# One of four weight combinations of a crossed MLP unit: accumulating transfer in place of a VectorE subtraction

## The chip, the cores and the metric

The kernel runs on one core of one Trainium2 chip. The metric is the device time of one execution in microseconds, median of several runs; smaller is better.

## What is computed

One block of a hybrid encoder on a sequence of 256 tokens with a model width of 2048: normalisation, one wide projection, a two-directional state-space branch and an attention branch, a gated merge, and then an MLP:

```
h2 = rms_norm(x, g_mlp)
x  = x + jnp.square(jax.nn.relu(h2 @ w_mlp_in)) @ w_mlp_out      # 2048 -> 8192 -> 2048
return rms_norm(x, g_final)
```

Everything is float32. The change touches only the product with `w_mlp_out` (8192 x 2048).

## The kernel before

**Pieces and blocks.** All weights stream from HBM in pieces of 128 partitions x 1024 floats (512 KB). SyncE (SP) issues the loads in one order (L610), in the MLP into a ring of seven raw buffers (`raw` and the second half of `gates`). For each block of weights ScalarE (ACT) writes a rounded copy, the high part, into `whi` or `whi_late` (L637), and VectorE (DVE) writes what is left, the low part, into `wlo` or `wlo_late` (L1022). TensorE (PE) then makes three products: high x high, high x low, low x high (L1719 to L1721; in the first MLP product, L1728 and L1732). There are eight slots for high and low parts, so ACT can be at most seven blocks ahead of PE: it waits on `used`, which PE increments after each block.

**The MLP.** The 8192 hidden columns are taken in four groups g. In each group four windows `mlp_in` make 2048 hidden columns, then windows `mlp_pair` multiply them into the output columns: q = 0 is the first half of the output columns, q = 1 the second; in the last group q = 1 is replaced by two plain windows. A column pair (g, q) has four units, each of 2 x 2 weight pieces: b11, b12, b22, b21 in load order. An ordinary unit has four blocks of 12 matmuls each. A **crossed** unit does the product of the 2 x 2 blocks with seven products in place of eight (Strassen's scheme in Winograd's form): the blocks are b11, b22, t1, b21, t3, t2, t4 (`PAIR_BLOCKS`), of six matmuls each, and t1 to t4 are combinations of the pieces:

```
t1 = b12 - b11    t3 = b22 - b12    t2 = b22 - t1    t4 = b21 - t2
```

`CROSSED` names the crossed units: units 1 and 2 with q = 0; units 0, 1 and 2 with q = 1. That makes 4 x 2 + 3 x 3 = 17 crossed units. With q = 1 the order is: half of unit 3, unit 0, unit 1, a quarter of unit 3, unit 2, the last quarter of unit 3.

DVE makes the four combinations (`difference`, L1025), in place, between its low parts; t1 overwrites b11, t3 overwrites b12, t2 overwrites b22, t4 overwrites b21. The order of DVE in a unit is: low b11, t1, low b22, t3, low t1, t2, low b21, t4, low t3, low t2, low t4. ACT makes the high parts in block order; before that of a combination it waits for `t_made`. The order on each engine is written out: `DUE` says at which step which block's parts are made, and the side work of a window (the copies of sums out of PSUM among it) stands between them.

**When a raw buffer is free.** `released(n)` says after how many low parts (`lo_made`) SP may load again into the buffer of piece n: `BLOCK[n] + (4, 5, 6, 7)[part]` for the four parts of a crossed unit. SP issues in the order of the pieces.

**The hidden side.** For the crossed units the sums of the hidden blocks are made by DVE in `hidden` (L1483 to L1490, `s_sum`), and after a column pair the product sums are combined (`mixed`, `mix_out`). ACT's `mix_out` copies the accumulated sums out of PSUM (L967) when PE has finished the last crossed unit of a column pair (for q = 1 between two high parts of the same step); after q = 1 PE waits for the first half of this copy (`m_out`) before it starts the next group's first `mlp_in` block in these banks. `carry_out` (L954) is a similar copy after q = 0.

GpSimd (POOL) has no work between the start of the MLP and the two last roots (L1622), and issues no transfer.

Of the kernel before, what the change touches and what calls it, by code (L numbers as in the profile page):

```python
# [23 lines left out]
ALU = mybir.AluOpType  # L24
# [105 lines left out]
MIX_OUT = {0: 4, 1: 5}  # L130
PAIR_PARTS = ((0, 0), (0, 1), (1, 1), (1, 0))
PAIR_FROM = {"b11": 0, "b22": 2, "b21": 3}
SUM_INTO = {"t1": 0, "t3": 1, "t2": 2, "t4": 3}
SUM_TURN = {"t1": 1, "t3": 2, "t2": 3, "t4": 4}
PAIR_BLOCKS = ("b11", "b22", "t1", "b21", "t3", "t2", "t4")


# [48 lines left out]
def released(n):  # L186

    if not crossed(n):
        return BLOCK[n] + 1
    part = pair_place(n)[3]  # L190
    return BLOCK[n] + (4, 5, 6, 7)[part]


def piece_number(r, par, p):
# [67 lines left out]
def build(nc, x, x_t, w_in, w_dt, gains_in, taps_in, rows_in, w_ssm_up, w_attn_up, w_out, w_mlp_in, w_mlp_out,  # L262
# [154 lines left out]
    def sem(name):  # L417
        return keep.enter_context(nc.semaphore(name))
# [51 lines left out]
    t_made, s_v, s_hi_made, s_lo_made = sem("t_made"), sem("s_v"), sem("s_hi_made"), sem("s_lo_made")  # L470
# [27 lines left out]
    def mix_bank(q, i):  # L498

        return (G if q else S)[:, i, :]  # L500
# [131 lines left out]
    def _(act):  # L632
# [6 lines left out]
        def split(m):  # L639
            n, i = SOURCE[m]  # L640
            if i is None:
                act.wait_ge(landed[piece_slot(n)], landings(n))
                high_part(m, n)
                return
            g, q, unit, _ = pair_place(n)
            turn = 4 * crossed_before(g, q, unit)
            block = PAIR_BLOCKS[i]
            if block in PAIR_FROM:
                n += PAIR_FROM[block]
                act.wait_ge(landed[piece_slot(n)], landings(n))  # L650
            else:
                n += SUM_INTO[block]
                act.wait_ge(t_made, turn + SUM_TURN[block])
            high_part(m, n)

        def split_high(rnd, dst, k0, gain=None, factor=1.0):
# [362 lines left out]
    def _(dve):  # L1019
# [1 line left out]
            dve.wait_ge(hi_made, m + 1)  # L1021
            dve.tensor_tensor(low(m), piece(n), high(m).bitcast(F32), ALU.subtract).then_inc(lo_made, 1)  # L1022

        def difference(n, of, less):
            dve.tensor_tensor(piece(n), piece(of), piece(less), ALU.subtract).then_inc(t_made, 1)  # L1025

        def split(m):
            n, i = SOURCE[m]
            if i is None:
                low_part(m, n)  # L1030
                return
            g, q, unit, _ = pair_place(n)
            turn = 4 * crossed_before(g, q, unit)
            if i == 0:
                low_part(m, n)
            if i == 1:
                dve.wait_ge(landed[piece_slot(n + 1)], landings(n + 1))
                dve.wait_ge(lo_made, m)
                difference(n, n + 1, n)
                low_part(m, n + 2)  # L1040
            if i == 2:
                difference(n + 1, n + 2, n + 1)
                low_part(m, n)
                dve.wait_ge(lo_made, m)
                difference(n + 2, n + 2, n)
            if i == 3:
                low_part(m, n + 3)
                dve.wait_ge(t_made, turn + 3)
                dve.wait_ge(lo_made, m + 1)
                difference(n + 3, n + 3, n + 2)  # L1050
            if i > 3:
                low_part(m, n + i - 3)

        def split_low(rnd, hi, lo, k0, gain=None, factor=1.0):

# [409 lines left out]
        def hidden(p, idx, pr, pp):  # L1465
            g, j = idx
            if p == 0:
                dve.wait_ge(hid_t, g * 4 + (j + 1))
                if 4 * g + j:
                    dve.wait_ge(hid_lo, g * 4 + j)  # L1470
                dve.wait_ge(hid_hi, g * 4 + (j + 1))
                dve.tensor_tensor(hidden_u, hidden_t, hidden_banks(j)[:, :, 0:T], ALU.add).then_inc(h_taken, 1)
                dve.wait_ge(h_taken, g * 4 + (j + 1))
                dve.scalar_tensor_tensor(out=hidden_u, in0=hidden_u, scalar=0.0,
                                         in1=rstd_row[:, :].unsqueeze(1).to_broadcast([P, 4, T]),
                                         op0=ALU.max, op1=ALU.mult).then_inc(hid_v, 1)
            if p == 2:
                dve.wait_ge(hid_hi, g * 4 + (j + 2))
                dve.tensor_tensor(b_lo[:, 4 * j:4 * j + 4, :], hidden_u,
                                  b_hi[:, 4 * j:4 * j + 4, :].bitcast(F32), ALU.subtract).then_inc(hid_lo, 1)  # L1480
            if p == 3 and j in SUMMED:
                a11, a12 = hidden_u[:, 0:2, 0:P], hidden_u[:, 2:4, 0:P]
                a21, a22 = hidden_u[:, 0:2, P:T], hidden_u[:, 2:4, P:T]  # L1483
                turn = 4 * (len(SUMMED) * g + j)
                dve.tensor_tensor(s_sum[:, 0, :, :], a21, a22, ALU.add).then_inc(s_v, 1)
                dve.tensor_tensor(s_sum[:, 2, :, :], a11, a21, ALU.subtract).then_inc(s_v, 1)
                dve.wait_ge(s_v, turn + 1)
                dve.tensor_tensor(s_sum[:, 1, :, :], s_sum[:, 0, :, :], a11, ALU.subtract).then_inc(s_v, 1)
# [20 lines left out]
        def mixed(p, idx, pr, pp):  # L1509
            g, q = idx  # L1510
            turn = 2 * g + q
            m, own = m_acc[q], x_sb[:, 2 * q:2 * q + 2, :, :]
            if p == 4:
                dve.wait_ge(m_out, 2 * turn + 2)
                dve.tensor_tensor(m[:, 1, :], m[:, 0, :], m[:, 1, :], ALU.add).then_inc(mix_v, 1)
                dve.wait_ge(mix_v, 4 * turn + 1)
                dve.tensor_tensor(m[:, 2, :], m[:, 1, :], m[:, 2, :], ALU.add).then_inc(mix_v, 1)
            if p == 6:
                if q:
                    dve.wait_ge(c_taken, 4 * g + 4)  # L1520
                else:
                    dve.wait_ge(c_added, g + 1)
                dve.wait_ge(mix_v, 4 * turn + 2)
                dve.tensor_tensor(own[:, 0, :, :], own[:, 0, :, :], m[:, 0:4:2, :], ALU.add).then_inc(mix_v, 1)
                dve.wait_ge(mix_v, 4 * turn + 3)
                dve.tensor_tensor(m[:, 1:3, :], m[:, 1:3, :], m[:, 3, :].unsqueeze(1).to_broadcast([P, 2, N]), ALU.add
                                  ).then_inc(mix_v, 1)
            if p == 7:
                dve.wait_ge(mix_v, 4 * turn + 4)
                dve.tensor_tensor(own[:, 1, :, :], own[:, 1, :, :], m[:, 1:3, :], ALU.add).then_inc(x_mixed, 1)  # L1530

        def mix_out(p, idx, pr, pp):
            g, q = idx
            if g == 3 and p == MIX_OUT[q]:
                dve.wait_ge(mix_a, 1)
                for i, (out_ap, of, bank) in enumerate(((mt[:, 1, 1, :], mt[:, 0, 0, :], 1), (mt[:, 0, 1, :], mt[:, 1, 1, :], 2),
                                                        (mt[:, 1, 0, :], mt[:, 1, 1, :], 3), (mt[:, 1, 1, :], mt[:, 0, 1, :], 3))):
                    if i in (1, 3):
                        dve.wait_ge(mix_v, 24 + i)
                    dve.tensor_tensor(out_ap, of, mix_bank(q, bank), ALU.add).then_inc(mix_v, 1)  # L1540
# [76 lines left out]
    def _(pool):  # L1617
# [555 lines left out]
```

## Time and profile before

| | us |
|---|---|
| median of 3 runs | 1622.39 |
| lowest, highest | 1622.16, 1622.67 |
| span of the profiled execution | 1620.0 |
| PE busy in it | 1608.5 |
| DVE busy | 1264.1 |
| ACT busy | 917.1 |
| POOL busy | 79.1 |

The span runs from the first to the last instruction of the program; the run's time is a little more. The profile lists, for each engine, when each instruction ran, and what ended the idle time before it. Times in the rows are microseconds from the start of the span. An instruction of DVE that follows another one without a wait starts before the other's recorded end: durations are 1.22 us, the pace is 1.14 us.

### The profile page before, as it was taken

Reading aid. Unit: us, or ns where it says so; the run is one execution under the profiler, and the core shown is the slowest. Engines: PE = TensorE matmul, PEld = TensorE weight load, DVE = VectorE, ACT = ScalarE, POOL = GpSimd, SP = SyncE. Lnnn points to the kernel's source line nnn. Section 1 sums busy time; section 2 is a strip of 40 time slices with the busy share of each in tenths; the row PEclk is TensorE's granted clock in tenths of the full one; section 3 lists DMA queues with packets and bytes.
Section 4 is the critical chain, followed back from the end, with each engine's and each line's share of the span. In section 5 each row is a group of like instructions: output and inputs, shape, how many; then the busy total and the mean of one; then the engine's idle time right before and its main releaser. Section 6 shows DMA issues by size and latency. Waiting matters only on the chain.

```text
span 1620.0 us, 20751 instructions
## 1 busy us (share of the span) xinstructions
PE 1608.5 (99%) x8104; PEld 1362.2 (84%) x8104; DVE 1264.1 (78%) x1520; ACT 917.1 (57%) x1262; POOL 79.1 (5%) x67
## 2 busy tenths in 40 slices
PE   9999999999999999999999999999999999999998
PEld 7888888888888888888888888888888888888886
DVE  7888878888666677776665576999799988998893
ACT  6666556666565445544444555665556556655562
POOL 3000000000001134000000000000000000000000
PEclk9999999999999999999999999999999999999999
DMA  7666665666556664445576676458646764586471
GB/s 272 202 200 190 189 200 189 208 195 203 183 186 182 191 187 153 142 145 175 187 229 195 225 236 187 144 182 285 184 125 224 262 190 134 194 282 209 148 245 53
DMA packets 134194, 312.21 MB, mean 193 GB/s; under 512 B 9744, under 2 KB 10448, under 8 KB 133968
## 3 DMA queue, kind: packets, MB, share of 16 engines
q1 hardware_dynamic: 129376, 302.21, 58.4%
q10 hardware_dynamic: 4720, 8.68, 2.0%
q8 instruction: 64, 1.05, 0.3%
q14 instruction: 34, 0.28, 0.0%
HBM read 308.68 MB, written 2.16 MB: 192 GB/s over the span
## 4 chain that ended last, share of the span: by engine, by line
PE 96%; DVE 2%; issue 1%; ACT 0%; POOL 0%; DMA 0%; POOLq 0%; DVEq 0%
PE G L1719 17%; PE G L1720 17%; PE G L1721 17%; PE G L1728 13%; PE S L1728 7%; PE G L1732 6%; PE S L1719 4%; PE S L1721 4%; PE S L1720 4%; PE S L1732 4%; PE S L1740 1%; PE S L1847 1%; DVE wlo L1022 1%; PE S L1891 0%; PE S L1824 0%
## 5 line engine op out<-in xcount | busy, mean ns | idle before, releaser
L637 ACT ACTIVATE whi<-raw 128x1024 fp32r<-128x1024 f32 x395 | 417.0, 1059 | 418.1 <-PE G L1721 254.9
L1022 DVE TENSOR_TENSOR wlo<-raw,whi 128x1024 fp32r<-128x1024 f32 x395 | 482.5, 1236 | 128.7 <-ACT whi L637 127.4
L1719 PE MATMUL G<-whi,a_both 128*128 128x512 f32 x768 | 301.3, 392 | 2.3 <-DVE wlo L1022 1.7
L1721 PE MATMUL G<-whi,a_both 128*128 128x512 f32 x768 | 299.5, 390 | 0.0
L1720 PE MATMUL G<-wlo,a_both 128*128 128x512 f32 x768 | 299.5, 390 | 0.0
L1728 PE MATMUL G<-a_both,whi 128*128 128x512 f32 x640 | 201.7, 397 | 0.0
L1719 PEld LDWEIGHTS G<-whi,a_both 128*128 128x128 f32 x768 | 144.3, 188 | 33.3 <-issue 2.6
L1721 PEld LDWEIGHTS G<-whi,a_both 128*128 128x128 f32 x768 | 144.2, 188 | 30.1
L1720 PEld LDWEIGHTS G<-wlo,a_both 128*128 128x128 f32 x768 | 144.3, 188 | 28.7
L1732 PEld LDWEIGHTS G<-a_both,wlo 128*128 128x128 f32 x640 | 120.3, 188 | 28.2
L1719 PE MATMUL G<-whi,b_hi 128*128 128x512 f32 x342 | 133.9, 392 | 0.0
L1720 PE MATMUL G<-wlo,b_hi 128*128 128x512 f32 x342 | 133.6, 391 | 0.0
L1721 PE MATMUL G<-whi,b_lo 128*128 128x512 f32 x342 | 133.3, 390 | 0.0
L637 ACT ACTIVATE whi_late<-raw 128x1024 fp32r<-128x1024 f32 x85 | 88.9, 1058 | 67.2 <-PE S L1732 22.0
L1732 PE MATMUL G<-a_both,wlo 128*128 128x256 f32 x640 | 125.9, 278 | 0.0
L1022 DVE TENSOR_TENSOR wlo_late<-raw,whi_late 128x1024 fp32r<-128x1024 f32 x85 | 102.6, 1221 | 24.7 <-ACT whi_late L637 24.1
L637 ACT ACTIVATE whi_late<-gates 128x1024 fp32r<-128x1024 f32 x67 | 70.0, 1056 | 49.7 <-PE G L1732 17.9
L1728 PEld LDWEIGHTS G<-a_both,whi 128*128 128x128 f32 x640 | 97.6, 189 | 0.1
L1022 DVE TENSOR_TENSOR wlo_late<-gates,whi_late 128x1024 fp32r<-128x1024 f32 x67 | 81.1, 1221 | 18.7 <-ACT whi_late L637 18.6
L637 ACT ACTIVATE whi<-gates 128x1024 fp32r<-128x1024 f32 x63 | 66.2, 1056 | 38.2 <-PE G L1732 13.9
L1022 DVE TENSOR_TENSOR wlo<-gates,whi 128x1024 fp32r<-128x1024 f32 x63 | 76.3, 1222 | 12.5 <-ACT whi L637 12.0
L1728 PE MATMUL G<-a_both,whi_late 128*128 128x512 f32 x256 | 80.5, 396 | 0.0
(306 smaller groups left out, 2692.4 us busy)
## 6 DMA issues: line engine op xcount, KB each, us to landing
raw<-in_w_in SPq DMA_DIRECT2D x208, 512.0 KB, 4.3
raw<-in_w_mlp_in SPq DMA_DIRECT2D x74, 512.0 KB, 4.0
raw<-in_w_mlp_out SPq DMA_DIRECT2D x74, 512.0 KB, 5.0
gates<-in_w_mlp_in SPq DMA_DIRECT2D x54, 512.0 KB, 4.0
gates<-in_w_mlp_out SPq DMA_DIRECT2D x54, 512.0 KB, 4.9
raw<-in_w_ssm_up SPq DMA_DIRECT2D x32, 512.0 KB, 3.8
raw<-in_w_attn_up SPq DMA_DIRECT2D x32, 512.0 KB, 4.6
raw<-in_w_out SPq DMA_DIRECT2D x32, 512.0 KB, 4.6
```

Source lines behind the costliest of these rows:

```text
L637: act.activation(high(m), piece(n), ACT.Copy).then_inc(hi_made, 1)
L1022: dve.tensor_tensor(low(m), piece(n), high(m).bitcast(F32), ALU.subtract).then_inc(lo_made, 1)
L1719: pe.matmul(out_ap, hi[:, k, cols], w_hi, start=start, stop=False)
L1720: pe.matmul(out_ap, hi[:, k, cols], w_lo, start=False, stop=False)
L1721: return pe.matmul(out_ap, lo[:, k, cols], w_hi, start=False, stop=stop)
L1728: pe.matmul(banks[:, c, :], high(m)[:, cols[kk]], a_both[:, 2 * p + kk, :, :].rearrange("p h t -> p (h t)"), start=(p + kk == 0), stop=False)
L1732: last = pe.matmul(banks[:, c, 0:T], low(m)[:, cols[kk]], a_hi[:, 2 * p + kk, :], start=False, stop=(2 * p + kk == KT - 1))
L1740: last = pe.transpose(S[:, c // 2, c % 2 * T + tb * P:c % 2 * T + (tb + 1) * P], src(c, tb), ident[:, :])
L1847: last = pe.matmul(S[:, 2, (4 * c + h) * HD:(4 * c + h + 1) * HD], mw[:, 0, h, c, :], tm[:, c, h * HD:(h + 1) * HD], start=True, stop=True)
```

## The change

The signs of the combinations are turned so that they are all additions:

```
t1 = b11 + b12    t3 = b12 + b22    t2 = t1 + b22    t4 = b21 + t2
```

The sums of the hidden blocks and the mixes after the products get the matching signs: add and subtract are swapped, with the same operands and shapes. t1, t2 and t4 stay DVE instructions (L1036, L1039 and L1043 in the changed file), at other places: t1 right behind low b11, t2 right behind low t1, t4 right behind low b21. t2 now overwrites b11's buffer, in which t1 stood, in place of b22's. t3 is made by a transfer that POOL issues (`add_blocks`): it adds b22's buffer onto b12's, once t1 is made and b22 has landed. Each combination has a semaphore of its own; t3's is incremented by 16 when the transfer has landed, and ACT waits for that before the high part of t3. The release of the raw buffers changes from (4, 5, 6, 7) to (6, 5, 5, 7).

```diff
-SUM_INTO = {"t1": 0, "t3": 1, "t2": 2, "t4": 3}
-SUM_TURN = {"t1": 1, "t3": 2, "t2": 3, "t4": 4}
+SUM_INTO = {"t1": 0, "t3": 1, "t2": 0, "t4": 3}
+SUM_STEP = {"t1": 1, "t3": 16, "t2": 1, "t4": 1}
...
-    return BLOCK[n] + (4, 5, 6, 7)[part]
+    return BLOCK[n] + (6, 5, 5, 7)[part]
...
-                act.wait_ge(t_made, turn + SUM_TURN[block])
+                act.wait_ge(sum_made[block], SUM_STEP[block] * (crossed_before(g, q, unit) + 1))
...
-        def difference(n, of, less):
-            dve.tensor_tensor(piece(n), piece(of), piece(less), ALU.subtract).then_inc(t_made, 1)
...
-            if i == 0:
-                low_part(m, n)
-            if i == 1:
+            low_part(m, n + (PAIR_FROM[block] if block in PAIR_FROM else SUM_INTO[block]))
+            b11, b12, b22, b21 = (piece(n + part) for part in range(4))
+            if block == "b11":
                 dve.wait_ge(landed[piece_slot(n + 1)], landings(n + 1))
-                dve.wait_ge(lo_made, m)
-                difference(n, n + 1, n)
-                low_part(m, n + 2)
-            if i == 2:
-                difference(n + 1, n + 2, n + 1)
-                low_part(m, n)
-                dve.wait_ge(lo_made, m)
-                difference(n + 2, n + 2, n)
-            if i == 3:
-                low_part(m, n + 3)
-                dve.wait_ge(t_made, turn + 3)
                 dve.wait_ge(lo_made, m + 1)
-                difference(n + 3, n + 3, n + 2)
-            if i > 3:
-                low_part(m, n + i - 3)
+                dve.tensor_tensor(b11, b11, b12, ALU.add).then_inc(sum_made["t1"], 1)
+            if block == "t1":
+                dve.wait_ge(lo_made, m + 1)
+                dve.tensor_tensor(b11, b11, b22, ALU.add).then_inc(sum_made["t2"], 1)
+            if block == "b21":
+                dve.wait_ge(lo_made, m + 1)
+                dve.wait_ge(sum_made["t2"], turn)
+                dve.tensor_tensor(b21, b21, b11, ALU.add).then_inc(sum_made["t4"], 1)
...
+        def add_blocks(n):
+
+            g, q, unit, _ = pair_place(n)
+            b12, b22 = piece(n + 1), piece(n + 2)
+            pool.wait_ge(sum_made["t1"], crossed_before(g, q, unit) + 1)
+            pool.wait_ge(landed[piece_slot(n + 2)], landings(n + 2))
+            pool.dma_start(b12, b22, accum_op=ALU.add).then_inc(sum_made["t3"], 16)
...
+                n = piece_number(r, par, p)
+                if crossed(n) and pair_place(n)[3] == 0:
+                    add_blocks(n)
```

What it does to the order, first on DVE, for unit 2 with q = 1 of the first group (L1022 is a low part, L1025 a difference). Before:

```order
760 L1022 TENSOR_TENSOR wlo_late<-gates,whi_late 128x1024
761 L1025 TENSOR_TENSOR gates<-gates 128x1024
762 L1022 TENSOR_TENSOR wlo_late<-gates,whi_late 128x1024
763 L1025 TENSOR_TENSOR gates<-gates 128x1024
764 L1022 TENSOR_TENSOR wlo<-gates,whi 128x1024
765 L1025 TENSOR_TENSOR gates<-gates 128x1024
766 L1022 TENSOR_TENSOR wlo<-raw,whi 128x1024
767 L1025 TENSOR_TENSOR raw<-raw,gates 128x1024
768 L1022 TENSOR_TENSOR wlo<-gates,whi 128x1024 x2
769 L1022 TENSOR_TENSOR wlo_late<-raw,whi_late 128x1024 x4
```

and now:

```order
755 L1022 TENSOR_TENSOR wlo_late<-gates,whi_late 128x1024
756 L1036 TENSOR_TENSOR gates<-gates 128x1024
757 L1022 TENSOR_TENSOR wlo_late<-gates,whi_late 128x1024
758 L1022 TENSOR_TENSOR wlo<-gates,whi 128x1024
759 L1039 TENSOR_TENSOR gates<-gates 128x1024
760 L1022 TENSOR_TENSOR wlo<-raw,whi 128x1024
761 L1043 TENSOR_TENSOR raw<-raw,gates 128x1024
762 L1022 TENSOR_TENSOR wlo<-gates,whi 128x1024 x2
763 L1022 TENSOR_TENSOR wlo_late<-raw,whi_late 128x1024 x4
```

The second difference is gone; five instructions in place of six stand between the end of t1 and the low part of t3.

On POOL, the whole stretch between the MLP's first root and the last two roots, before:

```order
48 L1622 TENSOR_TENSOR rstd_mlp<-x_var,minus_half 128x2 [waits var_x]
49 L1622 TENSOR_TENSOR rstd_out<-x_var,minus_half 128x1 [waits fin_sum] x2
```

and now its first rows, of 17 such transfers:

```order
48 L1614 TENSOR_TENSOR rstd_mlp<-x_var,minus_half 128x2 [waits var_x]
49 L1696 DMA raw<-raw 128x1024 [waits landed3,sum_t1_made]
50 L1696 DMA gates<-raw 128x1024 [waits landed0,sum_t1_made]
51 L1696 DMA raw<-raw 128x1024 [waits landed3,sum_t1_made]
52 L1696 DMA gates<-raw 128x1024 [waits landed0,sum_t1_made]
```

Each transfer waits for t1 and for b22's load; one moved to POOL per crossed unit, and nothing else did.

## Rows read from the trace of the kernel before

**Rows 1.** The page's parts 1 and 2: busy time and tenths of it in 40 slices.

```profile
PE 1608.5 (99%) x8104; PEld 1362.2 (84%) x8104; DVE 1264.1 (78%) x1520; ACT 917.1 (57%) x1262; POOL 79.1 (5%) x67
...
PE   9999999999999999999999999999999999999998
...
PEclk9999999999999999999999999999999999999999
```

**Rows 2.** PE's waits, first and last of four: us in total, times, longest.

```profile
PE G L1719 <- DVE wlo L1022: 1.7, 2, 1.3
...
PE S L1740 <- DVE tmp_a L1370: 0.2, 1, 0.2
```

**Rows 3.** Stretch: us, busy (count) of PE, PEld, DVE, ACT, POOL; clock, DMA.

```profile
980.00:1612.40 632.40, 632.40 (x3200) 537.29 (x3198) 546.32 (x521) 365.71 (x374) 0.93 (x1) 1.00 0.59 191
```

**Rows 4.** The same for line L1025 alone: us, DVE busy (count), clock, DMA.

```profile
1000.00:1600.00 600.00, 83.11 (x68) 1.00 0.59 193
```

**Rows 5.** Timeline of DVE, first group: start, us, instruction, idle before it.

```profile
1041.39 1.22 DVE L1022 TENSOR_TENSOR wlo_late<-gates,whi_late 128x1024 fp32r<-128x1024 f32 x1
...
1052.58 1.23 DVE L1022 TENSOR_TENSOR wlo<-raw,whi 128x1024 fp32r<-128x1024 f32 x1
...
1067.28 1.23 DVE L1022 TENSOR_TENSOR wlo_late<-gates,whi_late 128x1024 fp32r<-128x1024 f32 x1 [1.31 <-ACT whi_late L637]
1068.61 1.23 DVE L1025 TENSOR_TENSOR gates<-gates 128x1024 f32<-128x1024 f32 x1
...
1076.75 1.22 DVE L1022 TENSOR_TENSOR wlo<-gates,whi 128x1024 fp32r<-128x1024 f32 x1
...
1090.77 1.22 DVE L1022 TENSOR_TENSOR wlo<-gates,whi 128x1024 fp32r<-128x1024 f32 x1
```

**Rows 6.** Timeline of PE, where t3 starts (q = 0, then unit C) and the next group.

```profile
1045.52 0.39 PE L1719 MATMUL S<-whi_late,s_hi 128*128 128x512 f32 x1
...
1093.12 0.39 PE L1719 MATMUL G<-whi,s_hi 128*128 128x512 f32 x1
1093.35 0.39 PE L1720 MATMUL G<-wlo,s_hi 128*128 128x512 f32 x1
...
1099.92 0.62 PE L1728 MATMUL G<-a_both,whi_late 128*128 128x512 f32 x2
```

**Rows 7.** Timeline of ACT around unit A, and the copy after unit C.

```profile
1060.68 1.94 ACT L954 ACTIVATE tmp_both<-G 128x1024 f32<-128x1024 f32 x2 [1.60 <-PE G L1721]
1062.51 1.06 ACT L637 ACTIVATE whi_late<-raw 128x1024 fp32r<-128x1024 f32 x1
1063.46 1.06 ACT L637 ACTIVATE whi_late<-gates 128x1024 fp32r<-128x1024 f32 x1
1066.18 1.06 ACT L637 ACTIVATE whi_late<-gates 128x1024 fp32r<-128x1024 f32 x1 [1.66 <-PE S L1721]
...
1097.40 1.94 ACT L967 ACTIVATE m_acc<-G 128x1024 f32<-128x1024 f32 x2 [0.56 <-PE S L1721]
```

**Rows 8.** SP's issues, and loads' time to landing; the third is from 1061.15.

```profile
1043.78 0.37 SPq L610 DMA_DIRECT2D raw<-in_w_mlp_out  x1
raw<-in_w_mlp_out SPq DMA_DIRECT2D x1, 512.0 KB, 6.4
...
1050.59 0.37 SPq L610 DMA_DIRECT2D gates<-in_w_mlp_out  x1
gates<-in_w_mlp_out SPq DMA_DIRECT2D x1, 512.0 KB, 7.3
...
raw<-in_w_mlp_out SPq DMA_DIRECT2D x1, 512.0 KB, 3.5
...
1089.55 0.37 SPq L610 DMA_DIRECT2D raw<-in_w_mlp_in  x1
...
1092.02 0.37 SPq L610 DMA_DIRECT2D gates<-in_w_mlp_in  x1
```

**Rows 9.** Timeline of POOL near the end: a root on one element a partition.

```profile
1603.20 0.93 POOL L1622 TENSOR_TENSOR rstd_out<-x_var,minus_half 128x1 f32<-128x1 f32 x1 [658.16 <-DVE x_var L1603]
```

More of the change, by code:

```diff
@@ L469, in build @@
     row_mm = sem("row_mm")
-    t_made, s_v, s_hi_made, s_lo_made = sem("t_made"), sem("s_v"), sem("s_hi_made"), sem("s_lo_made")
+    sum_made = {block: sem(f"sum_{block}_made") for block in SUM_INTO}
+    s_v, s_hi_made, s_lo_made = sem("s_v"), sem("s_hi_made"), sem("s_lo_made")
     h_taken, c_taken = sem("h_taken"), sem("c_taken")
@@ L645, in split @@
             g, q, unit, _ = pair_place(n)
-            turn = 4 * crossed_before(g, q, unit)
             block = PAIR_BLOCKS[i]
@@ L1032, in split @@
             g, q, unit, _ = pair_place(n)
-            turn = 4 * crossed_before(g, q, unit)
-            if i == 0:
-                low_part(m, n)
-            if i == 1:
+            block, turn = PAIR_BLOCKS[i], crossed_before(g, q, unit) + 1
+            low_part(m, n + (PAIR_FROM[block] if block in PAIR_FROM else SUM_INTO[block]))
+            b11, b12, b22, b21 = (piece(n + part) for part in range(4))
+            if block == "b11":
                 dve.wait_ge(landed[piece_slot(n + 1)], landings(n + 1))
-                dve.wait_ge(lo_made, m)
-                difference(n, n + 1, n)
-                low_part(m, n + 2)
-            if i == 2:
-                difference(n + 1, n + 2, n + 1)
-                low_part(m, n)
-                dve.wait_ge(lo_made, m)
-                difference(n + 2, n + 2, n)
-            if i == 3:
-                low_part(m, n + 3)
-                dve.wait_ge(t_made, turn + 3)
-                dve.wait_ge(lo_made, m + 1)
-                difference(n + 3, n + 3, n + 2)
-            if i > 3:
-                low_part(m, n + i - 3)
+                dve.wait_ge(lo_made, m + 1)
+                dve.tensor_tensor(b11, b11, b12, ALU.add).then_inc(sum_made["t1"], 1)
[6 more added lines that the diff above has]
+                dve.tensor_tensor(b21, b21, b11, ALU.add).then_inc(sum_made["t4"], 1)
         def split_low(rnd, hi, lo, k0, gain=None, factor=1.0):
@@ L1484, in hidden @@
                 turn = 4 * (len(SUMMED) * g + j)
-                dve.tensor_tensor(s_sum[:, 0, :, :], a21, a22, ALU.add).then_inc(s_v, 1)
-                dve.tensor_tensor(s_sum[:, 2, :, :], a11, a21, ALU.subtract).then_inc(s_v, 1)
+                dve.tensor_tensor(s_sum[:, 0, :, :], a21, a22, ALU.subtract).then_inc(s_v, 1)
+                dve.tensor_tensor(s_sum[:, 2, :, :], a21, a11, ALU.subtract).then_inc(s_v, 1)
                 dve.wait_ge(s_v, turn + 1)
-                dve.tensor_tensor(s_sum[:, 1, :, :], s_sum[:, 0, :, :], a11, ALU.subtract).then_inc(s_v, 1)
+                dve.tensor_tensor(s_sum[:, 1, :, :], a11, s_sum[:, 0, :, :], ALU.subtract).then_inc(s_v, 1)
                 dve.wait_ge(s_v, turn + 3)
@@ L1514, in mixed @@
                 dve.wait_ge(m_out, 2 * turn + 2)
-                dve.tensor_tensor(m[:, 1, :], m[:, 0, :], m[:, 1, :], ALU.add).then_inc(mix_v, 1)
+                dve.tensor_tensor(m[:, 1, :], m[:, 0, :], m[:, 1, :], ALU.subtract).then_inc(mix_v, 1)
                 dve.wait_ge(mix_v, 4 * turn + 1)
-                dve.tensor_tensor(m[:, 2, :], m[:, 1, :], m[:, 2, :], ALU.add).then_inc(mix_v, 1)
+                dve.tensor_tensor(m[:, 2, :], m[:, 1, :], m[:, 2, :], ALU.subtract).then_inc(mix_v, 1)
             if p == 6:
@@ L1525, in mixed @@
                 dve.wait_ge(mix_v, 4 * turn + 3)
-                dve.tensor_tensor(m[:, 1:3, :], m[:, 1:3, :], m[:, 3, :].unsqueeze(1).to_broadcast([P, 2, N]), ALU.add
+                dve.tensor_tensor(m[:, 1:3, :], m[:, 1:3, :], m[:, 3, :].unsqueeze(1).to_broadcast([P, 2, N]), ALU.subtract
                                   ).then_inc(mix_v, 1)
@@ L1529, in mixed @@
                 dve.wait_ge(mix_v, 4 * turn + 4)
-                dve.tensor_tensor(own[:, 1, :, :], own[:, 1, :, :], m[:, 1:3, :], ALU.add).then_inc(x_mixed, 1)
+                dve.tensor_tensor(own[:, 1, :, :], own[:, 1, :, :], m[:, 1:3, :], ALU.subtract).then_inc(x_mixed, 1)
         def mix_out(p, idx, pr, pp):
@@ L1535, in mix_out @@
                 dve.wait_ge(mix_a, 1)
[L1536 to L1540, printed above, removed]
+                dve.tensor_tensor(mt[:, 1, 1, :], mt[:, 0, 0, :], mix_bank(q, 1), ALU.subtract).then_inc(mix_v, 1)
+                dve.wait_ge(mix_v, 25)
+                dve.tensor_tensor(mt[:, 0, 1, :], mt[:, 1, 1, :], mix_bank(q, 2), ALU.subtract).then_inc(mix_v, 1)
+                dve.tensor_tensor(mt[:, 1, 0, :], mix_bank(q, 3), mt[:, 1, 1, :], ALU.subtract).then_inc(mix_v, 1)
+                dve.wait_ge(mix_v, 27)
+                dve.tensor_tensor(mt[:, 1, 1, :], mix_bank(q, 3), mt[:, 0, 1, :], ALU.subtract).then_inc(mix_v, 1)
                 dve.wait_ge(mix_v, 28)
```

## The prediction

> **What bounds the kernel now.** I read the page first. TensorE (PE) is busy 1608.5 us of the 1620.0 us span, at full granted clock in all 40 slices [rows 1]. The list of waits of PE has four entries, 3.9 us together, the longest 1.5 [rows 2]. The stretch table for 980 to 1612.4 us, which holds the whole MLP, shows PE busy for 632.40 of 632.40 us, at clock 1.00 [rows 3]. What stands outside it is the tail after the last product, 1620.0 - 1612.4 = 7.6 us, which the change leaves alone. So no edit on VectorE (DVE), ScalarE (ACT) or a DMA can give anything back: each is worth something only as long as PE would otherwise wait for it, and it doesn't. The whole question is whether the change makes PE wait.
>
> PE is close to waiting at one place. In a crossed unit PE needs 6 x 0.227 = 1.36 us for a block (matmuls start 0.227 us apart [rows 6]). DVE, per unit of seven blocks, makes seven low parts and four differences, 11 instructions at a pace of 1.14 us: 12.5 us against 9.5 us of PE. So its lead over PE drains. The second column pair (q = 1) has three crossed units; I call them A, B and C, in the order 0, 1, 2. At block t3 of unit C in the first group DVE ends the low part at 1090.77 + 1.22 = 1091.99 us [rows 5] and PE starts on it at 1093.12 us [rows 6]: 1.1 us of lead is left. The second column pair occurs in three of the four groups.
>
> **The change part by part.**
>
> *Differences to additions, and the signs in the sums and mixes.* Same operands, shapes and engines; an add for a subtract. Cost 0. Nothing hides it, since nothing is added.
>
> *One DVE instruction less per crossed unit.* Before, there are 68 of these combinations, 83.11 us [rows 4], four in each of 17 units. 17 go: 17 x 1.22 = 20.8 us of DVE work. All of it lay beside PE work, so it is worth 0 us of the end directly; it is lead. How much lead: the low part of t3 in unit B starts at 1076.75, and 8 instructions stand before it from 1067.28 [rows 5]. Now seven do, but t1, t2 and t4 each wait for the low part just ahead, and such a wait shows as a step of 1.33 instead of 1.14 us (1067.28 to 1068.61). I get 1075.87: 0.88 us earlier, not 1.14.
>
> *The accumulating transfer.* t3 = b12 + b22 becomes a transfer issued by GpSimd (POOL) after t1 is made and b22 has landed. Behind the waiting POOL instruction stand only the next such transfers and the two small roots at the end. ACT waits for its landing, then makes the high part of t3 (1.06 us); behind that wait stand the high parts of t2, t4 and of the next unit, and the copies of the sums. Let L be the time from the end of the t1 addition to the landing. No row shows an accumulating transfer or any issued by POOL. Nearest rows: a plain load of the same 512 KB, little in flight, lands in 3.5 us; in a train of loads, landings follow each other (1050.59 + 7.3 - 1043.78 - 6.4) / 6 = 1.28 us apart [rows 8]. So 3.5 us holds about 1.3 us of data. Lower bound 3.5 us: the cheapest load. Upper bound 8.7 us: the slowest load of such a train, 7.3 us, and 1.3 us more data. What I take: 3.5, less SP's issue 0.37, plus 0.93 for POOL to write it (the nearest POOL row is its fixed cost on one element [rows 9]), plus 1.3 us because the transfer reads two buffers, plus 1.3 us for one load that it shares the queues with (units A and C fall into trains of loads). **L = 6.7 us**, an estimate.
>
> Here the Trainium skill speaks both ways. "DMA: Bandwidth & Descriptors", section "Anatomy of one DMA", fits a POOL transfer as 2.0 us + bytes / 436 GB/s, an estimate of 3.2 us for 512 KB; "Collectives: The Full Stack", section "The bandwidth ceiling", says of a transfer that adds that it is slower since it needs "two source reads", and halves the rate. No row here shows either. By the first alone nothing of the change would be seen; by the second my doubled data stands.
>
> *What L costs, place by place, first group.*
>
> Unit A. Its t1 sum ends at about 1052.58 + 1.33 + 1.23 = 1055.1 [rows 5]. ACT then has, in order, high t3, the two copies of L954, high t2, high t4 and the next unit's first high, which starts 0.95 + 1.83 + 0.95 + 0.95 = 4.7 us after high t3, at 1059.8 + L. Today it starts at 1066.18, since it waits for PE to free its slot [rows 7]. Free up to L = 6.4; at 6.7, 0.3 us late.
>
> Unit B. The t1 sum ends at 1068.61 + 1.23 = 1069.84. Low t3 could start at 1075.87, and starts at 1069.84 + L + 1.09. So DVE stalls L - 4.94 = 1.76 us.
>
> Unit C. The same: 1.76 us. Its low t3 ends at 1091.99 - 2 x 0.88 + stalls = 1090.23 + stalls.
>
> Against PE at t3 that leaves 1093.12 - 1090.23 = 2.9 us for the stalls. But something stands later and is tighter. *The slots' release is changed:* b11's buffer is free after the low part of t2 instead of that of b21. Piece 370, the first such load after unit C, is issued at 1089.55 today, when low b21 ends, and piece 371 at 1092.02, when low t3 ends [rows 8]; SP issues in order. Now 370 waits for low t2, 1.14 us after low t3, and 371 goes right behind it. 371 lands 3.5 + 1.28 us later; ACT makes its high part (1.06), and only then comes ACT's copy of unit C's sums out of PSUM (L967, 1097.40 today), whose first half (1.0) PE waits for before the block that starts at 1099.92 [rows 6, 7]. From the end of low t3: 1.14 + 3.5 + 1.28 + 1.06 + 1.0 + 0.1 = 8.1 us. That leaves 1099.92 - 8.1 - 1090.23 = 1.6 us for the stalls.
>
> Sum per group: 0.3 + 1.76 + 1.76 - 1.6 = 2.2 us of PE wait. Three groups: 6.7 us. The first column pair (q = 0) has two crossed units; at its t3, low ends at 1042.61 and PE starts at 1045.52 [rows 5, 6], 2.9 us of lead and 0.88 gained: free up to L = 8.7 us. Cost 0.
>
> On the profile's own span: 1620.0 + 6.7 = 1626.7. The median of the runs is 2.4 us above it, so **1629.1 us**.
>
> **The rivals.**
>
> 1. *The cover holds, no change.* If L stays under 5.7 us, 2 x (L - 4.94) is under 1.6 and PE never waits: 1622.4 us. Up to L = 6.3 the cost is at most 3 x (2 x 1.34 - 1.6) = 3.2 us, 0.2%. For it: the lone load's 3.5 us, and one data stream instead of two gives L = 5.4. Against: the shared queues. This is the side other than my forecast; it decides at 5.7 us. The skill's fit named above would end here, at an estimated L of 3.2.
>
> 2. *The transfer is slow.* An adding transfer of 8.7 us: per group 2.3 + 3.76 + 3.76 - 1.6 = 8.2 us, three times 24.7, 1647 us. Beyond it the first column pair joins, four times L - 8.7: at 10 us, 3 x 12.1 + 5.2 = 42 us, 1664 us. For it: no row bounds it from above. Against: no load takes over 7.3 us here.
>
> 3. *DVE's relief buys time, faster.* That needs a PE wait in the MLP that goes, and rows 2 and 3 show none: the most is a fraction of 3.9 us, and none of those stands near the units. 1622 us at best.
>
> 4. *The transfer doesn't run beside the rest* (POOL held up or its transfers one behind another). Units are some 12 us of DVE apart and POOL is idle in the MLP, 0.93 us busy [rows 3], so only L could show it: case 2.
>
> **How the numbers follow.** By L: under 5.7 us (rival 1, lossless) 0.28; 5.7 to 7.5 us (my forecast, PE waits at the end of unit C) 0.47, of which 0.12 costs under 3.2 us and 0.35 costs 3.2 to 14 us; over 7.5 us (rivals 2 and 4) 0.22; rival 3, 0.03. The forecast is the likeliest. Faster by over 0.2% (3.2 us, about what a measurement of this kernel can tell from no change): 0.03. Within it: 0.28 + 0.12 = 0.40. Slower: 0.35 + 0.22 = 0.57. The range goes from 1621.8, no change with its scatter, to 1650 us, rival 2 at its first bound and a little beyond; about 0.1 of slower cases is left out.
>
> **What would show each step.** In the trace of after: 51 DVE combinations, not 68, and 17 transfers on a POOL queue whose time to landing is L less the issue. ACT's high t3 should begin at the landing, and the low part of t3 in units B and C stand alone, with an idle DVE before it of L - 4.9. PE's waits should be at the first block after unit C, released by ACT's copy L967, three times, none with q = 0. If PE's waits name low t3 itself, my step from low t3 to the copy is too long. If PE's list of waits stays as it is, L was under 5.7, and I was wrong on the two reads or the sharing. A landing over 8 us with waits in all seven column pairs is rival 2.

## The result and the profile after

| | before | after |
|---|---|---|
| median, us | 1622.43 | 1651.49 |
| lowest, highest | 1622.16, 1622.67 | 1649.14, 1654.53 |
| span of the profiled execution | 1620.0 | 1649.1 |
| ratio, 95% interval | | 1.018 [1.0169, 1.0192] |

The changed kernel takes 29 us more. The forecast was 1629.1, its range ended at 1650.0.

The page of after, busy time and the share of the transfers' queue (packets, MB, share of 16 engines' span), beside [rows 1]:

```profile
PE 1617.1 (98%) x8104; PEld 1365.0 (83%) x8104; DVE 1250.1 (76%) x1503; ACT 913.9 (55%) x1262; POOL 94.2 (6%) x84
PE   9999999999999999999999999989998999989998
q0 software_dynamic: 2448, 8.91, 2.7%
```

PE makes the same 8104 matmuls but is recorded busy 8.6 us longer, and idle 20.5 us longer (32.0 against 11.5): together the 29.1 us of the span. DVE has 17 instructions less and is no help. Three dips to 8 have come in PE's row, one in each group that has a second column pair.

PE's waits in after (us in total, times, longest), where before had two of 1.7 us together on this line [rows 2]:

```profile
PE G L1722 <- DVE wlo L1022: 20.0, 8, 4.9
PE G L1722 <- issue: 1.7, 3, 0.7
```

And where they stand, the timeline of PE in the first group, at t3 of unit B and of unit C; compare the undisturbed 1093.12 of [rows 6]:

```profile
1083.53 0.51 PE L1722 MATMUL G<-whi,s_hi 128*128 128x512 f32 x1 [2.06 <-DVE wlo L1022]
...
1100.66 0.80 PE L1722 MATMUL G<-whi,s_hi 128*128 128x512 f32 x1 [4.44 <-DVE wlo L1022]
1101.25 0.63 PE L1723 MATMUL G<-wlo,s_hi 128*128 128x512 f32 x1
1101.67 0.63 PE L1724 MATMUL G<-whi,s_lo 128*128 128x512 f32 x1
...
1109.03 0.70 PE L1731 MATMUL G<-a_both,whi_late 128*128 128x512 f32 x2
```

The next group's first block, at 1099.92 before [rows 6], starts at 1109.03: 9.1 us are lost in this group. The same block is 19.5 us late in the second group and 28.9 in the third, so the loss is 9.1, 10.4 and 9.3 us, and next to nothing is lost elsewhere.

Why low t3 is late: the transfers as POOL issues them in units A, B and C (the number after the start is the issue itself on POOL), and below, for each in turn, the median time to landing of the issues in a stretch that holds only that one:

```profile
1057.20 0.87 POOL L1696 DMA_DIRECT2D raw<-raw  x1 [21.63 <-DVE raw L1036]
1072.39 0.88 POOL L1696 DMA_DIRECT2D gates<-raw  x1 [14.32 <-DVE gates L1036]
1089.71 0.86 POOL L1696 DMA_DIRECT2D gates<-gates  x1 [16.44 <-DVE raw L1036]
```

```profile
raw<-raw POOLq DMA_DIRECT2D x1, 512.0 KB, 6.0
...
gates<-raw POOLq DMA_DIRECT2D x1, 512.0 KB, 8.7
...
gates<-gates POOLq DMA_DIRECT2D x1, 512.0 KB, 8.6
```

The addition t1 ends 0.4 us before each issue, so L, the time from its end to the landing, was 6.4 us in A, 9.2 in B and 8.9 in C. All nine times from issue to landing with q = 1, A/B/C by group: 6.0/8.7/8.6, 6.9/8.2/8.6, 6.5/8.1/8.9. With q = 0 the eight took 4.4 to 5.6 us.

What stands in front of the transfers: SP's issues in after, first those ahead of unit B's transfer and then those ahead of unit C's:

```profile
1068.37 1.39 SPq L611 DMA_DIRECT2D raw<-in_w_mlp_out  x3
1069.81 0.47 SPq L611 DMA_DIRECT2D gates<-in_w_mlp_out  x1
...
1084.64 0.88 SPq L611 DMA_DIRECT2D gates<-in_w_mlp_out  x2
1085.56 0.47 SPq L611 DMA_DIRECT2D raw<-in_w_mlp_out  x1
1086.08 1.30 SPq L611 DMA_DIRECT2D raw<-in_w_mlp_in  x2
```

In before the first four of these loads spread over 4.8 us:

```profile
1061.15 4.07 SPq L610 DMA_DIRECT2D raw<-in_w_mlp_out  x3
1065.99 0.37 SPq L610 DMA_DIRECT2D gates<-in_w_mlp_out  x1
```

The release (6, 5, 5, 7) does it: b11's buffer now waits for the low part of t2, SP issues in order, and by then the buffers of b12 and b22 are free and that of b21 nearly. So four or five loads go out within 2.3 us, and they land 1.2 to 2.7 us apart: ahead of B's transfer at 1072.2, 1073.8, 1076.5 and 1077.7. The transfer, issued at 1072.4, has three of them in front and lands at 1081.1. In before the fourth had landed at 1071.4, 1.5 us after t1 was made. At unit C four of five are still to land when the transfer is issued, the first of them within 0.3 us and the last at 1095.8; the transfer lands at 1098.3. In A it lands at 1063.2, the last load at 1060.8. In all three it comes 2.4 to 3.4 us after the last load ahead of it. A's transfer had three loads in front too (landing at 1058.2, 1059.6 and 1060.8), but the last of them landed 3.6 us after its issue, against 5.3 in B and 6.1 in C.

The loads bunch without any transfer too. This is the same place in the first experiment below, which has the new release but makes t3 on DVE:

```profile
1067.30 1.39 SPq L611 DMA_DIRECT2D raw<-in_w_mlp_out  x3
1068.74 0.47 SPq L611 DMA_DIRECT2D gates<-in_w_mlp_out  x1
```

### The profile page after: what moved, and what is told of

Its sections match the earlier page's. It is cut to its first block, busy times and chain, and to the rows that moved or that the text cites. A ratio compares the mean times of both kernels' runs of the same rounds, so it can differ in the third digit from the quotient of the medians.

```text
span 1649.1 us, 20768 instructions
## 1 busy us (share of the span) xinstructions
PE 1617.1 (98%) x8104; PEld 1365.0 (83%) x8104; DVE 1250.1 (76%) x1503; ACT 913.9 (55%) x1262; POOL 94.2 (6%) x84
## 4 chain that ended last, share of the span: by engine, by line
PE 83%; DMA 7%; DVE 6%; ACT 2%; issue 1%; POOL 0%; POOLq 0%; SPq 0%; DVEq 0%; ACTq 0%
PE G L1722 15%; PE G L1723 15%; PE G L1724 15%; PE G L1731 13%; PE S L1731 7%; PE G L1735 6%; PE S L1735 4%; DMA raw<-raw 2%; PE S L1722 2%; PE S L1723 2%; DVE wlo L1022 2%; PE S L1724 2%; DVE wlo_late L1022 2%; DMA gates<-gates 1%; DMA gates<-raw 1%
## 5 line engine op out<-in xcount | busy, mean ns | idle before, releaser
L1022 DVE TENSOR_TENSOR wlo<-raw,whi 128x1024 fp32r<-128x1024 f32 x394 | 482.3, 1238 | 143.2 <-ACT whi L638 141.8
L1022 DVE TENSOR_TENSOR wlo_late<-raw,whi_late 128x1024 fp32r<-128x1024 f32 x86 | 104.0, 1222 | 31.0 <-ACT whi_late L638 30.3
L1022 DVE TENSOR_TENSOR wlo<-gates,whi 128x1024 fp32r<-128x1024 f32 x64 | 77.7, 1222 | 33.8 <-ACT whi L638 33.2
L1022 DVE TENSOR_TENSOR wlo_late<-gates,whi_late 128x1024 fp32r<-128x1024 f32 x66 | 80.2, 1221 | 19.3 <-ACT whi_late L638 19.3
```

## The experiments

The theory was: the slow landings cost it, through DVE and ACT, up to ACT's copy of unit C's sums (the two L967 instructions whose first half PE waits for before the next group); the transfer itself is short, and the loads that the new release bunches in front make it long. Rivals: the new release and order cost it without any transfer; the length comes from the two reads; the transfers with q = 0 have a share; PE's clock.

**t3 by VectorE, all else as after**

```diff
+            if block == "b22":
+                dve.wait_ge(sum_made["t1"], turn)
+                dve.tensor_tensor(b12, b12, b22, ALU.add).then_inc(sum_made["t3"], 16)
...
-                if crossed(n) and pair_place(n)[3] == 0:
-                    add_blocks(n)
```

> The changed kernel with one part undone: t3 = b12 + b22 is a VectorE addition behind the low part of b22, and no transfer is issued by GpSimd. The new order of the sums and the new release of the raw buffers (6, 5, 5, 7) stay. Theory (the late landing of the transfer makes TensorE wait): TensorE's waits in the MLP shrink to those at the copy after unit C, at most 0.5 us in each of three groups; 1622 to 1624.5 us. Rival (the later release of b11's buffer, and the loads that bunch up behind it, cost the time by themselves): high parts wait for loads, 1635 us or more.

1628.41 us (1627.11 to 1629.27), ratio 1.0037 [1.0025, 1.005]: near the theory's side, but 4 us above its range. PE's waits in it:

```profile
PE G L1732 <- ACT m_acc L967: 3.5, 3, 1.3
PE G L1723 <- DVE wlo L1022: 2.9, 4, 1.4
```

The transfer accounts for 23 us of the 29, release and order for 6. The first line is the wait that I had forecast for the changed kernel: the first block after unit C, for the copy L967, three times; but it is 1.2 us each time, where at most 0.5 was expected.

**Before with the late release of b11 alone**

```diff
-    return BLOCK[n] + (4, 5, 6, 7)[part]
+    return BLOCK[n] + (6, 5, 6, 7)[part]
```

> The kernel before with b11's raw buffer released after the low part of t2 instead of that of b21: (6, 5, 6, 7) for (4, 5, 6, 7). Nothing else. Theory (the new release is a cost of its own: the loads after unit C come later, and with them the high part that stands before ACT's copy of the sums, for which TensorE waits): TensorE waits on ACT's copy L967, about 1 us in each of three groups, perhaps with a fraction at t3; 1624 to 1629 us. Rival (the 6 us of the run with t3 on VectorE came from its new order on VectorE, not from the release): 1622.4 us.

1628.13 us (1627.05 to 1628.63), ratio 1.0036 [1.0023, 1.0048]; its waits:

```profile
PE G L1719 <- DVE wlo L1022: 3.2, 5, 1.3
PE G L1728 <- ACT m_acc L967: 2.7, 3, 1.2
```

The same time and much the same waits as the kernel above. The 6 us are the release's; signs and places of the additions cost nothing, as forecast.

**A transfer of 32 KB** (64 of the 1024 columns)

```diff
-            pool.dma_start(b12, b22, accum_op=ALU.add).then_inc(sum_made["t3"], 16)
+            pool.dma_start(b12[:, 0:64], b22[:, 0:64], accum_op=ALU.add).then_inc(sum_made["t3"], 16)
```

> The changed kernel with the adding transfer cut to 64 of 1024 columns (32 KB), the rest of t3's sum left out; the same waits, the same number of transfers. Theory (sharing packet by packet: a transfer with few packets gets through a train of loads quickly): landing about 2 to 3 us when alone and 3 to 5 us for B and C; no wait of TensorE beyond 0.5 us a group; 1622 to 1624.5 us. Rival (first come, first served: the transfer starts only when the loads ahead are done): landing for B and C 5.5 us or more, 1630 us or more.

1623.68 us (1623.15 to 1625.81), ratio 1.0011 [1.0002, 1.0021]. Landings with q = 1: 3.5 to 6.6 us, at the shortest elsewhere 2.2. The time is in the theory's range; of the landings in unit C two (5.7 and 6.6 us) are beyond the rival's mark of 5.5. With short landings the change would cost 1.5 us. That is 4.7 us less than the first experiment with the same release and order: the one DVE instruction less per unit is worth something after all, as soon as the late release has made DVE's chain bind.

**A plain copy in place of the addition**

```diff
-            pool.dma_start(b12, b22, accum_op=ALU.add).then_inc(sum_made["t3"], 16)
+            pool.dma_start(b12, b22).then_inc(sum_made["t3"], 16)
```

> The changed kernel with a plain copy of b22 over b12 by the same GpSimd transfer, in place of the addition, so t3 is not the sum. Its 4 KB packets should take about 159 ns as the plain loads' do, not 328. Theory (data of the transfer counts doubly, alone and in sharing): landings for B and C fall from some 8.6 to 6 to 7 us, the lone ones from 4.4 to 3.1; 1628 to 1638 us. Rival (only the position in the queue behind the loads counts): landings fall by at most 0.7 us and the time stays at 1645 or more.

1637.15 us (1635.92 to 1637.35), ratio 1.0091 [1.0076, 1.0106]. PE's longest group of waits, and the queue's line on the page:

```profile
PE G L1722 <- DVE wlo L1022: 10.7, 5, 3.5
...
q0 software_dynamic: 2448, 8.91, 1.3%
```

The same packets and bytes take 1.3% in place of 2.7% of the engines' time: the added read doubles it. Undisturbed a copy lands in 2.8 us, an addition in 4.4. Of these 1.6 us, 0.3 are the issue on POOL (0.53 us for a copy, 0.87 for an addition) and 1.3 are left for the second read. The copy takes 6.8 to 8.3 us in B and 7.1 to 7.7 in C: longer than the theory's 6 to 7, though the time is in its range. So a plain copy of 512 KB costs 13.5 us more than the addition of 32 KB (from 1623.7 to 1637.2), and the addition of 512 KB 14.3 more than the copy. An estimated 3 us of these 14.3 are the longer issue (0.34 us in three units of three groups), the rest I put down to the second read, alone and in the trains.

**Loads held back until t3 has landed** (with q = 1, units B and C)

```diff
+                if n - 4 >= N_MLP and crossed(n - 1) and pair_place(n - 1)[3] == 3 and pair_place(n - 1)[1] == 1:
+                    g0, q0, unit0, _ = pair_place(n - 1)
+                    if unit0:
+                        sp.wait_ge(sum_made["t3"], 16 * (crossed_before(g0, q0, unit0) + 1))
```

> The changed kernel, but SyncE waits, with q = 1 after the last load of units B and C (its own b21), until that unit's t3 has landed before it issues the next load. Three of the four loads that stood ahead of B's transfer (and three or four at C) are so moved behind it. Theory (the transfer shares the DMA engines with a train of loads): time from issue to landing for B and C falls from 8.1 to 8.9 us to about 4.5 to 5.5, like the transfers that meet no loads (4.4); 1622 to 1626 us. Rival (an adding transfer is slow by itself there, whatever the loads do): landing stays above 7 us and the time at 1645 or more, since the loads are now later as well.

1639.41 us (1637.46 to 1641.1), ratio 1.0106 [1.0091, 1.0121]. The time to landing in unit B and then in unit C of the first group:

```profile
gates<-raw POOLq DMA_DIRECT2D x1, 512.0 KB, 5.9
...
gates<-gates POOLq DMA_DIRECT2D x1, 512.0 KB, 4.4
```

In the other two groups 4.4 us in all four places; A, which was left alone, keeps its 6.0 to 6.9. The same transfer of the same bytes takes half as long once the loads are away from it: that settles what made it long. The time misses the forecast of 1622 to 1626 us all the same. The price is that the held loads come late, and PE's waits move to them and to the copy:

```profile
PE G L1735 <- ACT m_acc L971: 5.5, 3, 2.0
PE G L1726 <- DVE wlo L1026: 3.8, 6, 1.3
PE G L1726 <- issue: 3.4, 3, 2.1
```

12 us are won, 17 stay. No run has the transfers with q = 1 under the old release, so what the release costs through the longer landings is not separated from the transfer's own cost.

**Transfers with q = 0 only** (with q = 1 places and release of before)

```diff
+    return BLOCK[n] + ((4, 5, 6, 7) if q else (6, 5, 5, 7))[part]
...
+                if crossed(n) and pair_place(n)[3] == 0 and pair_place(n)[1] == 0:
+                    add_blocks(n)
```

> Transfers in the eight crossed units with q = 0 alone, with the changed kernel's order and release there; with q = 1 the four sums are VectorE additions in the places, the buffers and with the release (4, 5, 6, 7) of the kernel before. Theory (the transfer costs nothing where the lead is over 3 us, and all of the loss arises with q = 1): landings 4.4 to 5.9 us as there, TensorE's list of waits like that of the kernel before, 1622 to 1623 us. Rival (part of the loss is spread over all transfers, by GpSimd or by traffic): some 8/17 of 29 us, 1630 us or more.

1622.51 us (1622.03 to 1623.15), ratio 1.0002 [0.9993, 1.0011]. Eight transfers, landing in 4.4 to 5.3 us, cost nothing where PE's lead is about 3 us or more and two units stand side by side in place of three.

**Transfers with q = 1 only** (with q = 0 places and release of before)

```diff
+    return BLOCK[n] + ((6, 5, 5, 7) if q else (4, 5, 6, 7))[part]
...
+                if crossed(n) and pair_place(n)[3] == 0 and pair_place(n)[1] == 1:
+                    add_blocks(n)
```

> Transfers only with q = 1 (units A, B, C, nine of them); with q = 0 the combinations, their places and the release (4, 5, 6, 7) are those of before. Theory, the sum with measured terms: in the changed kernel the sum t1 of unit A ends at 1056.84 us in the first group, 1.7 us later than before, only because the later release with q = 0 bunches the loads ahead of it, and the 9.1 us that PE loses per group contain these 1.7 in full, since everything from that sum to the next group's first block is one chain (landing, high parts, DVE, landing, DVE, landing, two loads, copy). With q = 0 as before it should end at 1055.1, and each group lose about 7.4 us: 3 x 1.7 = 5 us less than the changed kernel, 1646.3 us (1645 to 1648.5), with the landings of B and C unchanged at 8 to 9 us. Rival: the chain starts anew at the loads of B and C, so that A's start doesn't matter, or the transfers with q = 0 and the relief of DVE there weigh for themselves: 1650 to 1653 us, as the changed kernel.

1646.22 us (1645.59 to 1647.73), ratio 1.0148 [1.0131, 1.0165]: the time that the sum with measured terms gave, 5 us under the changed kernel. The t1 addition of unit A is back where it stood before (1053.93 in this run, 1053.91 in before, 1055.61 in after):

```profile
1053.93 1.23 DVE L1066 TENSOR_TENSOR raw<-raw 128x1024 f32<-128x1024 f32 x1
```

So the release with q = 0 costs nothing by itself but delays the start of a chain that has no slack left. The 5 us are not evenly spread as I had expected, though. The three groups gain 0.5, 2.5 and 1.3 us in place of 1.7 each, so that the total came out so exactly is in part luck. In the first, t3 of unit C lands 1.1 us earlier and the copy of the sums starts 1.3 us earlier (1106.68 against 1107.94), but PE's next group starts only 0.5 us earlier (1108.57 against 1109.03). There PE ran on a lower clock for longer than in after (0.66 against 0.83 over the same window, the number before the last two; more of this in the next experiment), and its own work set the end:

```profile
1095.00:1105.00 10.00, 5.59 (x16) 4.33 (x16) 6.76 (x6) 6.36 (x7) 0.00 (x0) 0.66 0.42 123
```

**PE kept at work while it waits for t3 of unit C** (16 products of zeros, added to a bank: the sums stay the same)

```diff
+                        if PAIR_BLOCKS[i] == "t3" and q == 1 and unit == 2:
+                            pe.wait_ge(zeroed, 1)
+                            for _ in range(16):
+                                pe.matmul(mix_bank(q, 1), zeros[:, :],
+                                          b_hi[:, 4 * unit:4 * unit + 2, :].rearrange("p k t -> p (k t)"),
+                                          start=False, stop=False)
```

> The changed kernel with 16 matmuls more in each of the three groups, of a matrix of zeros into an open sum, just before TensorE's wait for t3 of unit C (16 x 0.227 = 3.6 us of work that changes no result). Theory (the stretches at half clock of 3.4 to 6.8 us come from TensorE's idle stretch of some 4.4 us there): the idle stretch is under 1.5 us, the granted clock stays at its upper level (2.4 GHz) in the MLP, TensorE's waits at C shrink by 3.6 us each, and the time falls by 5 to 7 us, to 1644 to 1647 us, though TensorE has 11 us more work. Rival (the clock falls for another reason): the slow stretches stay and the time is 1651 us or more.

A miss: 1653.39 us (1652.32 to 1654.81), ratio 1.0193 [1.0179, 1.0207], no faster than the changed kernel. That is the rival's time, but not for the rival's reason: the slow stretches at unit C did go. The windows of after around unit C in the three groups (width; busy and count of PE, PEld, DVE, ACT, POOL; granted clock; DMA):

```profile
1095.00:1105.00 10.00, 5.56 (x19) 4.15 (x18) 6.39 (x6) 5.79 (x6) 0.00 (x0) 0.83 0.43 101
1275.00:1285.00 10.00, 5.97 (x17) 4.43 (x16) 6.79 (x7) 6.13 (x7) 0.00 (x0) 0.66 0.41 112
1455.00:1465.00 10.00, 5.86 (x19) 4.76 (x20) 6.90 (x6) 6.50 (x7) 0.00 (x0) 0.83 0.39 122
```

and with the fill (wider windows in the second and third group):

```profile
1095.00:1105.00 10.00, 10.00 (x46) 8.29 (x45) 6.32 (x6) 5.80 (x6) 0.00 (x0) 1.00 0.41 100
1270.00:1285.00 15.00, 13.83 (x61) 10.95 (x60) 10.97 (x10) 6.11 (x7) 0.00 (x0) 1.00 0.58 164
1450.00:1465.00 15.00, 12.86 (x55) 9.98 (x55) 10.57 (x11) 6.86 (x7) 0.00 (x0) 1.00 0.54 147
```

But the next group starts no earlier, now after a wait for the copy. In the first group:

```profile
1109.09 0.72 PE L1734 MATMUL G<-a_both,whi_late 128*128 128x512 f32 x2 [0.88 <-ACT m_acc L969]
```

1109.03 and 1109.09 are the same place. In after PE arrives there without a wait only because it was slow on the way. What sets the place is ACT's chain, the two high parts that wait for loads and the copy behind them, here in after:

```profile
1098.29 1.06 ACT L638 ACTIVATE whi<-gates 128x1024 fp32r<-128x1024 f32 x1 [6.68 <-DMA gates<-gates]
...
1105.72 1.06 ACT L638 ACTIVATE whi<-raw 128x1024 fp32r<-128x1024 f32 x1 [1.64 <-DMA raw<-in_w_mlp_in]
1106.97 1.06 ACT L638 ACTIVATE whi<-gates 128x1024 fp32r<-128x1024 f32 x1 [0.19 <-DMA gates<-in_w_mlp_in]
1107.94 1.92 ACT L967 ACTIVATE m_acc<-G 128x1024 f32<-128x1024 f32 x2
```

The lower clock lies under it. It shows only where the slow stretch is long, in the second group of after, at 0.66, which loses 10.4 us where the other two lose 9.1 and 9.3:

```profile
1286.88 1.92 ACT L967 ACTIVATE m_acc<-G 128x1024 f32<-128x1024 f32 x2
...
1288.87 0.62 PE L1731 MATMUL G<-a_both,whi_late 128*128 128x512 f32 x2
```

Where PE waits for this copy it starts 1.06 us after the copy does (1109.09 and 1108.04 in the first group with the fill). Here it starts 1.99 us after it, without a wait: 0.9 us late by its own slow work. With the fill the three groups lose 9.2, 9.9 and 11.1 us. In the second 0.5 us are won. In the third ACT gets the load of unit C's first piece 1.1 us later than in after, and the transfer of C takes 9.8 us in place of 8.9.

No version here is faster than before. PE has no idle time that these transfers could give back.

## Why the prediction was wrong

**Direction and mechanism: right.** The transfer is too slow for q = 1 and free for q = 0. The additions, the signs and DVE's 17 instructions are worth nothing by themselves while PE is the bound. The chain through DVE's stalls in B and C to the load 371, its high part and the copy L967 is the one that sets the end.

**L was the term that failed, and in it the sharing.** I had put 1.3 us for one load in front of the transfer; it measured 4.4 and 4.1 us in units B and C, with three or four loads in front. Term by term:

| first group | as predicted | measured |
|---|---|---|
| L of a lone transfer, without sharing | 5.4 | 4.8 (0.4 to the issue, 4.4 to landing) |
| added by loads in front: A | 1.3 | 1.6 |
| B | 1.3 | 4.4 |
| C | 1.3 | 4.1 |
| L in B and C | 6.7 | 9.2, 8.9 |

The two source reads were rightly taken: 1.3 us in my sum, and 1.3 us left between the lone copy and the lone addition. The Trainium skill's fit for one DMA ("DMA: Bandwidth & Descriptors", section "Anatomy of one DMA") gives an estimated 3.2 us for this size. The lone copy took 2.8 us and the lone addition 4.4, so the fit is near the copy and too short for the addition. The Trainium skill's "Collectives: The Full Stack", section "The bandwidth ceiling", says that an addition is slower for its "two source reads", at half the rate. The 2.7% against 1.3% of the engines' time agree with that.

The sharing was sized by one load of the old trains [rows 8]. I had seen that the new release holds the load 370 back to low t2 and lets 371 follow, but used that only after unit C. The same sentence holds at the end of each crossed unit: it puts three loads in front of the next unit's transfer.

**The steps from L on held.** The stall L - 4.94 (by my own steps of 1.33 and 1.14 us it should have been 4.90) gives 4.25 us for B and 3.97 for C. DVE stood idle for 4.30 in B, and in C for 0.40 and 3.61:

```profile
1082.25 1.23 DVE L1022 TENSOR_TENSOR wlo<-gates,whi 128x1024 fp32r<-128x1024 f32 x1 [4.30 <-ACT whi L638]
...
1089.74 1.23 DVE L1022 TENSOR_TENSOR wlo<-gates,whi 128x1024 fp32r<-128x1024 f32 x1 [0.40 <-ACT whi L638]
...
1099.38 1.23 DVE L1022 TENSOR_TENSOR wlo<-gates,whi 128x1024 fp32r<-128x1024 f32 x1 [3.61 <-ACT whi L638]
```

From the end of low t3 of unit C (1100.60) to the next group I had 8.1 us; it took 8.43.

**A second step failed, smaller: unit A's start.** I let its t1 addition end at 1055.1 as before. The release with q = 0 bunches loads there too, the load of b11 comes later, and it ended at 1056.84. B's first high part, forecast 4.7 us after t3's landing in A, started at 1067.92, which is 1063.23 + 4.7; before it was 1066.18. This 1.7 us goes through to the end, and grows to 2.1 at B's t1 addition (1070.72 against 1068.61 before), since DVE is still at another low part when B's first high part is ready.

**The sum with what was measured.** The terms are how late B's t1 addition starts, counted from the start of the group (1070.72, 1249.93 and 1429.52, against 1068.61, 1238.02 and 1407.43 before), the stalls of DVE in B and in C, 0.3 us for the longer copy path, and the cover of 1.6 us:

| group | B's start | B | C | copy path | cover | PE's own slow work | sum | lost |
|---|---|---|---|---|---|---|---|---|
| first | 2.1 | 4.3 | 4.0 | 0.3 | -1.6 | | 9.1 | 9.1 |
| second | 2.8 | 3.7 | 4.3 | 0.3 | -1.6 | 0.9 | 10.4 | 10.4 |
| third | 2.6 | 3.6 | 4.4 | 0.3 | -1.6 | | 9.3 | 9.3 |

The copy path was measured in the first group and is taken over for the other two. Together it is 28.8 of the 29 us.

**The signs.** As forecast: 51 combinations on DVE and 17 transfers, low t3 alone after an idle DVE, no wait at t3 with q = 0. Landings over 8 us came, but with q = 1 only, not with waits in all seven column pairs. Otherwise than forecast, PE waits for low t3 itself, in B and in C, and not for the copy at the first block after unit C (but for 0.1 us in the third group). I had read that sign in advance as a path from t3 to the copy that is too long, and that reading is wrong: the path was 0.3 us too short. With L at 9, PE must wait at t3 as well, since there the lead without stalls was only 2.9 us; the wait at t3 is inside the delay at the copy, not added to it. In the first experiment, without the transfer, the forecast place shows itself.

**The rivals.** Rival 2, the slow transfer, is what happened: at L = 8.7 it gave 1647 us, 4 under the result. Its chance of 0.22 was too low: I named an upper bound from the longest load of a train and then took a middle value, though the change itself lengthens the trains. Rival 1 needed L under 5.7, which is the lone case (4.8). Its bound of 3.2 us at L = 6.3 should read 3.4 (2 x 1.36), which changes nothing. The release was priced too low as well: by my sum it costs 3 x 0.2 us when DVE isn't relieved (8.1 us from 1091.99, against 1099.92) and nothing when it is; it costs 6 and 1.5 us (the runs with late release and with 32 KB). The path of 8.1 us is not to blame. In the run with the late release alone the low part of t3 of unit C starts at 1093.24, 2.5 us later than before, and the next group 8.1 us after its end:

```profile
1093.24 1.22 DVE L1022 TENSOR_TENSOR wlo<-gates,whi 128x1024 fp32r<-128x1024 f32 x1
...
1102.57 0.74 PE L1728 MATMUL G<-a_both,whi_late 128*128 128x512 f32 x2 [0.92 <-ACT m_acc L967]
```

What I had put at nothing is that the release also makes the units start later.

## What to carry to other kernels

A transfer that takes an instruction off an engine must be sized with the loads that stand in front of it in the changed kernel, not in the old one: if the change also moves a buffer's release, redraw the load issues around every place where the transfer runs. Where buffers are freed in order, holding back the first frees several at once, and the burst arrives just when the next short transfer wants the queues. And a PE wait that is easy to see, or a slow clock, can lie wholly under a later wait; filling or removing it shows that better than adding it up.

## What the runs showed of the hardware

- An accumulating transfer of 512 KB between SBUF buffers takes 2.1 times the engine time of a plain one (2.7% against 1.3%) and lands in 4.4 us alone; the plain one in 2.8 us, an accumulating one of 32 KB in 2.2 us. Of these times 0.87 us are the issue on POOL for an accumulating transfer, 0.53 for a plain one.
- Issued by POOL behind loads that SP has already issued, three or four of them not yet landed in the units of the first group, it lands 2.4 to 3.4 us after the last of them, though it is in another queue. It isn't strictly behind them: the 32 KB transfer of unit B landed at 1074.9, 0.2 us after the last load ahead of it (1074.7), and alone such a transfer takes 2.2 us. How the engines divide their time between the two queues, and how much of the delay is before the first packet, was not separated.
- PE ran on its lower level after waits: matmuls from 1101.25 on start 0.42 us apart (1.2 GHz) in place of 0.23 (2.4 GHz), after 4.44 us without work; the granted clock of the three windows is 0.83, 0.66 and 0.83. With the fill the one such stretch left in the MLP comes 1.3 us after the end of a wait of 2.1 us at t3 of unit B, though in after a wait of the same length there (2.06 us) left the clock at 1.00:

```profile
1085.00:1090.00 5.00, 5.00 (x17) 3.96 (x16) 4.49 (x5) 2.34 (x4) 0.19 (x1) 0.66 0.78 262
```

  In the kernel before it is 1.00 over the whole MLP [rows 3], and with PE kept at work at unit C it is 1.00 there.
